# Residual update of two of four token tiles moved from VectorE to ScalarE and GpSimd, in a decoder block on one Trainium2 core

## The reference, cut to what matters

```python
h = rms_norm(x, pre_g1[l]) * (1.0 + sc1) + sh1
y = token_mixing(h, ...)                              # attention and gated MLP, then @ w_out
x = x + gt1 * rms_norm(y, post_g1[l])                 # the residual update that the change touches
h = rms_norm(x, pre_g2[l]) * (1.0 + sc2) + sh2        # the rows that PEER reads
y = peer_ffn(h, ...)                                  # queries, top 16 per side, top 16 of pairs, experts
x = x + gt2 * rms_norm(y, post_g2[l])
```

## Time and profile before

| | us |
|---|---|
| median of 3 runs (1538.06 to 1541.35) | 1538.43 |
| the profiled execution's own time | 1538.31 |
| its span, first to last instruction | 1536.5 |
| PE busy, share of the span | 95% |
| DVE busy | 86% |
| POOL busy | 51% |
| ACT busy | 45% |

### The profile page before, as it was taken

The page is one execution under the profiler, slowest core; times in us unless marked ns, Lnnn a source line. Parts: engine busy times, 40 slices in busy tenths (PEclk is TensorE's granted clock), DMA queues, the critical chain, the costliest instruction groups (busy, mean ns, idle before and its releaser), DMA issues.

```text
span 1536.5 us, 25606 instructions
## 1 busy us (share of the span) xinstructions
PE 1461.5 (95%) x7921; PEld 1254.3 (82%) x7921; DVE 1324.6 (86%) x2653; ACT 691.0 (45%) x1383; POOL 782.7 (51%) x733
## 2 busy tenths in 40 slices
PE   7999999999989868889999999999999999999996
PEld 5777767867578667778999999999999989999985
DVE  5878645346999989798999999999999999999998
ACT  5232456322157657634444444444444444444443
POOL 1000000000059957677767767767767767667662
PEclk9999999999999989999999999999999999999998
DMA  9995111450021165899999999999999999999994
GB/s 344 352 383 194 61 56 56 145 187 1 1 110 51 64 246 232 339 401 402 401 400 401 401 392 403 401 380 400 401 377 402 397 378 402 399 383 401 395 384 161
DMA packets 164992, 448.85 MB, mean 292 GB/s; under 512 B 14683, under 2 KB 50675, under 8 KB 164284
## 3 DMA queue, kind: packets, MB, share of 16 engines
q1 hardware_dynamic: 108732, 243.33, 42.5%
q0 software_dynamic: 56192, 204.66, 33.9%
HBM read 423.72 MB, written 22.32 MB: 290 GB/s over the span
## 4 chain that ended last, share of the span: by engine, by line
PE 75%; DVE 16%; DMA 3%; issue 2%; ACT 2%; POOL 1%; SPq 0%; ACTq 0%; DVEq 0%; POOLq 0%
PE bank L954 15%; PE bank L1225 8%; PE bank L1224 8%; PE bank L1223 8%; PE bank L1246 7%; PE bank L1247 7%; PE bank L1248 7%; PE bank L1239 4%; PE bank L1238 4%; PE bank L1145 2%; PE bank L1058 2%; DMA w_scratch<-staged 1%; PE bank L897 1%; DVE top_i L1959 1%; DVE scores L1960 1%
## 5 line engine op out<-in xcount | busy, mean ns | idle before, releaser
L790 POOL DMA_INDIRECT v_rows<-v_exp,small x192 | 257.4, 1341 | 91.3 <-POOL small L786 51.8
L790 POOL DMA_INDIRECT u_rows<-u_exp,small x192 | 254.3, 1325 | 93.1 <-POOL small L786 52.0
L1223 PE MATMUL bank<-h_hi,u_hi 128*128 128x320 f32 x944 | 291.2, 308 | 0.7 <-ACT staged L1521 0.7
L1225 PE MATMUL bank<-h_hi,u_lo 128*128 128x320 f32 x944 | 291.7, 309 | 0.0
L1224 PE MATMUL bank<-h_lo,u_hi 128*128 128x320 f32 x944 | 291.5, 309 | 0.0
L1246 PE MATMUL bank<-v_hi,g_parts 128*128 128x512 f32 x512 | 200.0, 391 | 0.0
L1247 PE MATMUL bank<-v_lo,g_parts 128*128 128x512 f32 x512 | 199.5, 390 | 0.0
L1248 PE MATMUL bank<-v_hi,g_parts 128*128 128x512 f32 x512 | 199.4, 389 | 0.0
L1624 ACT ACTIVATE v_hi<-v_raw 128x1024 fp32r<-128x1024 f32 x128 | 135.3, 1057 | 117.9 <-PE bank L1248 106.1
L1223 PEld LDWEIGHTS bank<-h_hi,u_hi 128*128 128x128 f32 x944 | 177.2, 188 | 5.4 <-ACT staged L1521 0.9
L1224 PEld LDWEIGHTS bank<-h_lo,u_hi 128*128 128x128 f32 x944 | 177.2, 188 | 4.6
(11 more groups left out here) (257 smaller groups left out, 2965.6 us busy)
## 6 DMA issues: line engine op xcount, KB each, us to landing
v_raw<-v_exp SPq DMA_DIRECT2D x128, 512.0 KB
u_raw<-u_by_key SPq DMA_DIRECT2D x120, 512.0 KB
ada_blk<-ada_w SPq DMA_DIRECT2D x22, 1024.0 KB, 11.1
ring<-w_in SPq DMA_DIRECT2D x18, 1024.0 KB, 10.0
w_row<-w_scratch SPq DMA_DIRECT2D x128, 128.0 KB
w_scratch<-staged SPq DMA_DIRECT2D x2, 4096.0 KB, 17.8
xr<-x SPq DMA_DIRECT2D x8, 512.0 KB, 6.2
ring<-w_branch SPq DMA_DIRECT2D x4, 1024.0 KB, 5.0
```

Of the source, the lines that this page charges most:

```text
L790: pool.indirect_dma_start(out=rows[s], out_offset=None, in_=table, in_offset=bass.IndirectOffsetOnAxis(ap=ix[:, s:s + 1], axis=0))\
L1223: pe.matmul(o, u_hi[:, r, k], h2_hi[:, k], start=(k == 0), stop=False)
L1225: last = pe.matmul(o, u_lo[:, r, k], h2_hi[:, k], start=False, stop=(k == KD - 1))
```

## The change

`x_step(2)` and `x_step(3)` leave DVE. ACT gets `x_scale(t)`, one ACTIVATE behind `squares_of(1, t)`, which multiplies `nat` by the root. It waits for the root. POOL gets `x_step(t)`, two instructions behind `norm(1, t)`: a multiply of `nat` by `mod(2)` and an add into `xr`. It raises `x_moved`. ACT's `x_squares` and SP's store of `xr` wait for `x_moved` for those tiles. On DVE `h2_step(2)` moves from behind the first indices to behind the second MAX8, and `h2_step(3)` from behind the second indices to behind the index and replace of the sums. Before the CAST of `pick(1)` DVE now waits for the products of `mixer_out` (`group("y")`), which an earlier `x_step(3)` implied. The two semaphores `g_hi_done` and `g_half_done` become one with two counts a block.

```diff
-            sp.wait_ge(x_new, NT)
+            sp.wait_ge(x_new, 2)
+            sp.wait_ge(x_moved, NT - 2)
...
+            def x_step(t):
+
+                pool.wait_ge(x_scaled, t - 1)
+                pool.wait_ge(x_in[t], 32)
+                link(pool.tensor_tensor(nat[:, t, :], nat[:, t, :], mod(2), ALU.mult))
+                pool.tensor_tensor(xr[:, t, :], xr[:, t, :], nat[:, t, :], ALU.add).then_inc(x_moved, 1)
+
             for k, t in NORMS[2 * NT:3 * NT]:
                 norm(k, t)
+                if k == 1:
+                    x_step(t)
...
-                pe.wait_ge(g_half_done, j + 1)
+                pe.wait_ge(g_hi_done, j * 2 + 2)
...
+            def x_scale(t):
+                act.wait_ge(rstd_ready, NORM_NO[1, t])
+                act.activation(nat[:, t, :], nat[:, t, :], ACT.Copy, scale=rstd(1, t)).then_inc(x_scaled, 1)
+
             def x_squares(t):
-                act.wait_ge(x_new, t + 1)
+                if t < 2:
+                    act.wait_ge(x_new, t + 1)
+                else:
+                    act.wait_ge(x_moved, t - 1)
                 squares_of(2, t, xr[:, t, :], junk2)
...
             squares_of(1, 2, nat[:, 2, :], junk2)
+            x_scale(2)
             x_squares(2)
             mixer_out(3)
             squares_of(1, 3, nat[:, 3, :], junk2)
+            x_scale(3)
             picks_across(0)
             h2_across(2)
             x_squares(3)
...
-                act.activation(g_half(r), gated[:, r, DS - EX:DS], ACT.Copy).then_inc(g_half_done, 1)
+                act.activation(g_half(r), gated[:, r, DS - EX:DS], ACT.Copy).then_inc(g_hi_done, 1)
...
                     for n in some:
-                        if t == 1 and n == PH:
-                            x_step(2)
                         dve.max_index(top_i[:, n, 0:8], top[:, n, 0:8], side[n])
                         ins = dve.match_replace(side[n], top[:, n, 0:8], side[n], LOWEST)
                     tick(ins)
-                    if t == 1:
-                        h2_step(2)
                     settled()
...
                     if t == 1:
-                        x_step(3)
+                        h2_step(2)
                     settled()
...
-                if t == 1:
-                    h2_step(3)
                 settled()
                 dve.nop().then_inc(scores_read, 1)
+                if t == 1:
+                    multiplied(dve, *group("y"))
                 dve.tensor_copy(top_f, top_i)
...
                 tick(ins)
+                if t == 1:
+                    h2_step(3)
                 settled()
...
-                dve.wait_ge(g_hi_done, b + 1)
+                dve.wait_ge(g_hi_done, b * 2 + 1)
```

More of the change, by code:

```diff
@@ L489, in build @@
                              "exp_ready", "p_ready"))
+        x_scaled, x_moved = sem("x_scaled"), sem("x_moved")
         merged, x_new, h2_ready, idx_ready = (sem(n) for n in ("merged", "x_new", "h2_ready", "idx_ready"))
@@ L501, in build @@
                                         for n in ("u_raw_in", "v_raw_in", "w_row_in"))
-        u_hi_done, u_lo_done, v_hi_done, v_lo_done, a_full, gel_done, gated_done, g_hi_done, g_half_done, g_lo_done, v_done = (
+        u_hi_done, u_lo_done, v_hi_done, v_lo_done, a_full, gel_done, gated_done, g_hi_done, g_lo_done, v_done = (
             sem(n) for n in ("u_hi_done", "u_lo_done", "v_hi_done", "v_lo_done", "a_full", "gel_done",
-                             "gated_done", "g_hi_done", "g_half_done", "g_lo_done", "v_done"))
+                             "gated_done", "g_hi_done", "g_lo_done", "v_done"))
         y_full, y_squared, y_normed = sem("y_full"), sem("y_squared"), sem("y_normed")
```

## The result

The changed kernel takes 1543.59 us (median of 16 runs, 1541.48 to 1545.40). The kernel before, run beside it, took 1538.24 (16 runs, 1534.55 to 1543.26). The ratio is 1.0033, 95% interval 1.0024 to 1.0041: **5.1 us slower**, 3.7 to 6.3. The forecast was 1541.0, range 1537.4 to 1545.0. The direction and the main mechanism came out as written; the forecast's +2.7 us was 2.4 us too small. The profiled execution of the changed kernel took 1543.99 us, its span is 1542.0, 5.5 us longer than before.

What follows compares the result with a forecast made beforehand. The bound was taken as group 23 on GpSimd and the DMA behind it, not VectorE. From 1538.31, 0 from (a), (b), (c) and (h) and +2.7 from (d) to (f) gave 1541.0 us, range 1537.4 to 1545.0.

Steps and rivals of the forecast that it cites:

- the third stretch: VectorE's third COPY and COPY_PREDICATED spreading of picks, 530.67 to 537.83 before; forecast to begin at 525.8 plus d.
- (a): On VectorE, two steps fewer bring everything after 443.4 up to 4.9 us earlier, worth nothing by itself at 544.9.
- (b): On VectorE, the moved h2_step(3) again starts at about 436.1, plus 0.2 us for a wait; 0 in the sum.
- (c): Tile 3's new chain on ScalarE and GpSimd: multiply and add 2.5 us each, root at 435.8, before 436.3; 0.
- d: Delay of VectorE's CAST and all VectorE work behind it if it waits for GpSimd's add: 0 to 2.3 us.
- (d): VectorE reaches the CAST at 431.4 while GpSimd adds; whether it waits was left open, 0 to 2.3 us.
- (e): ScalarE's h2_across(2) waits behind x_scale(3); group 0 on PE starts at 446.7, 2.1 us late, absorbed by group 3.
- (f): VectorE's earlier spreading of picks slows GpSimd's group 23, which ends 1.1 to 4.6 us later; 2.7 taken.
- (g): After group 23, the DMA, h_hi, group 24, the store and the loop are in series and shift by the same amount.
- (h): Merged semaphore and SP's xr store: one more register value a block on PE and VectorE in the loop costs 0.
- the rival with the slow pair: GpSimd's multiply and add for tile 3 take 6.2 us each; kernel at 1543.3 to 1546, chance 0.10.

Runs made afterwards that it cites:

- the relief alone: The changed kernel with x_scale and GpSimd's multiply and add left out for tiles 2 and 3; 1540.82 us, ratio 1.0020 to the kernel before.
- the other order on ScalarE: The changed kernel with picks_across(0) and h2_across(2) ahead of x_scale(3) on ScalarE; 1543.07 us, ratio 1.0032 to the kernel before.
- the two kernels named under the table: The changed kernel without x_scale and GpSimd's multiply and add (1540.82 us); the changed kernel with CAST behind h2_step(3) and h2_across(2) ahead of x_scale(3) (1541.47 us).

## Why the prediction was right, and where it was short

The direction, the path through group 23 and the DMA, and the overlap with the third stretch were right. Group 23 was taken 2.7 us late and was 3.9 us late. The rest, some 1.2 us of the 5.1, lies behind group 23, where the sum had nothing.

- **What bounds the kernel:** right. VectorE's group 24 was early, and the DMA behind group 23 ended last. Holding VectorE back cost nothing, and moving the DMA brought 7.9 us to the changed kernel. In the kernel before the lead was smaller than the "at least 1.6 us": moving the DMA brought 1.0 us there, not clear of noise.
- **(a) The relief is worth nothing at 544.9:** right. The kernel with the relief alone was even 2.4 to 3.1 us slower than before, of which its trace shows 0.3 at group 23.
- **(b) and (c):** `h2_step(3)` was put at 436.3 plus d; it started at 438.50. GpSimd's pair takes 2.35 us each for the 2.5 estimated. The estimate from the figure that the Trainium skill gives (GPSIMD Engine Reference, elementwise cycle accounting), 4497 ns halved, was 2.25, and the trace agrees within 5%. `x_scale(3)` ran at 427.88 for 427.3, since the root ahead of it came at 427.85 for 427.2. The root after the pair came at 436.0 for 435.8.
- **(d) The CAST:** d was left between 0 and 2.3 and the sum took about the middle; it measured 2.2 (438.50 for 436.3). 1.6 of them are the CAST (1.90 for 0.29), 0.3 the wait ahead of it (0.52 for the 0.2 taken). The CAST ended 0.15 us behind the add. The Trainium skill (SBUF — State Buffer, who interferes with whom) has a cast in VectorE's two-port mode and a GpSimd instruction block each other for the whole instruction. By that rule the forecast had 1.8 to 2.3. The trace agrees with the rule; it gave 1.6, as the CAST started at 432.14 and not at 431.4.
- **(e) ScalarE's order:** the copy came at 429.30 (428.7 expected). The step that failed is the next one. Group 0 on PE was put at 446.7 and started at 449.84, because the queries took 17.40 us, not 14.53. PE had been idle for 1.65 and 2.73 us, and its granted clock was 0.50, the 1.2 GHz level, from 430 to 436 us (1.00 before). With the other order on ScalarE the second idle time was 0.78 us and the queries took 15.98, not the 14.5 expected of that run: the 1.65 us ahead of it were still there. The step also took groups 0 and 1 on GpSimd as unaffected. They wait for `h2_step(3)`, and group 0 came 2.4 us late (441.25 for 438.85). Group 23 started 1.6 us later than before (528.88 for 527.30).
- **(f) The third stretch on group 23:** right in kind, the main term. Group 23 ended 3.9 us later, inside the 1.1 to 4.6, above the 2.7 taken, and 6.2 us after the first COPY, within the 6.1 to 7.3 taken. The term was mis-sized by the start of the stretch: 528.50 is 2.7 us behind the 525.8 without any delay, beyond d's upper end of 2.3, while the sum took about the middle. The remaining 0.5 us behind d was not followed up. That the range held the time is in part luck: its upper end for this case, 1542.9, was passed, and 1545.0 came from the rival with the slow pair.
- **(g) All in series:** nearly. 3.9 us at group 23 are 4.3 at `h_hi`, 4.9 at the store of the gate matrix (607.70 for 602.84), 5.0 at the loop's load of `a_early` and 5.5 at the end. These steps are small beside the scatter of single executions, but the two kernels named under the table lose some 2 us there, so "by the same amount" is not shown to hold.
- **(h) The semaphore:** right, 1.0002. The reason given for it was not tested.

## What to carry to other kernels

An engine that is busy 97% of a stage and feeds the next one need not be its bound: look for what the consumer (here ScalarE) waits for last, and put its queue's oldest wait beside the chain. Before taking work off an engine that is early, ask what its instructions will now overlap; here VectorE's COPY and COPY_PREDICATED fell on the last rows that GpSimd had to make. When a relief brings nothing, move the transfer that covers it: the same change was a loss of 5.1 us with the DMA late, and a gain of 1.8 us with the DMA early in both kernels (1535.70 for 1537.55).

## What the runs showed of the hardware that was not expected

- A CAST of 128x256 on VectorE took 1.90 us instead of 0.29 while GpSimd ran a two-input add over 128x1024, and ended 0.15 us behind it.
- Four GpSimd instructions, 3.12 us together when alone, took 5.8 to 5.9 us among VectorE's COPY and COPY_PREDICATED in all seven profiles in which the third stretch caught the group whole, and 3.9 us where it caught the last one only (3.87 us, tile 3 back on VectorE).
- The same small instruction of GpSimd (`norm`, 128x1) took 0.49 us instead of 0.19 at 426.62 us, when VectorE ran TENSOR_TENSOR instructions over 128x384 and more.
- PE, idle for 1.65 and then 2.73 us, ran 128 small multiplies in 17.40 us instead of 14.53, at a granted clock of 0.50 from 430 to 436 us. After 1.66 and 0.78 us of idling they took 15.98 us.
